# Another dealing of the next tile's attention steps over the parts of the expert heads

## What is computed

```
# forgetting attention, per head (causal)
logits = q k^T * scale + fq[:, None] - log_fcum[None, :]
out = softmax(where(k_pos <= q_pos, logits, -inf)) v
# stick-breaking attention, per head
z = q k^T * scale
log_one_minus = where(k_pos < q_pos, log_sigmoid(-z), 0)
rest = reverse_cumsum(log_one_minus) - log_one_minus
out = where(mask, exp(log_sigmoid(z) + rest), 0) v
x = x + gt1 * (concat(norm(fox), norm(stick)) @ w_out)
# expert layer, per token t and expert head h
u = expert_down[e[t, h, 0:16]]          # gathered rows, by the ids
act = gelu(x u) * gate
x = x + gt2 * sum(act * expert_up[e[t, h, 0:16]])
```

## Time and profile before

| | us |
|---|---|
| three runs, median | 2913.8 |
| the profiled execution's own time | 2913.59 |
| its span in the trace | 2911.8 |
| A1 (30 parts), from 1461.62 | 154.3 |
| A2, from 1826.85 | 167.0 |
| A3, from 2201.24 | 167.4 |

### The profile page before, as it was taken

How to read it: one execution, slowest core, us unless ns; L and a number is a source line. 1 busy time by engine, 2 the same in 40 slices (tenths; PEclk the granted TensorE clock), 3 DMA queues, 4 the chain that set the end, 5 groups by cost and what they waited for, 6 DMA issues and landing times.

```text
span 2911.8 us, 29792 instructions
## 1 busy us (share of the span) xinstructions
PE 2233.5 (77%) x10060; PEld 1001.9 (34%) x10060; DVE 1537.3 (53%) x3500; ACT 840.6 (29%) x1822; POOL 591.3 (20%) x588
## 2 busy tenths in 40 slices
PE   5997999887878874999877667887668876675554
PEld 2444434532222222755632123422234322321110
DVE  3987843500000003201387676777667877677764
ACT  3105301110010002311255322764226652132221
POOL 1000000000000001000134333333333433344442
PEclk9999999898998997999977788988889988887768
DMA  9784545299999997122579999899998999999997
GB/s 369 269 196 131 184 161 232 106 387 405 411 415 404 407 406 302 46 71 76 193 288 411 420 415 421 339 378 411 413 421 348 386 401 407 421 421 421 421 421 294
DMA packets 155968, 948.43 MB, mean 326 GB/s; under 512 B 18522, under 2 KB 50312, under 8 KB 65982
## 3 DMA queue, kind: packets, MB, share of 16 engines
q0 software_dynamic: 78704, 556.90, 47.1%
q1 hardware_dynamic: 68224, 381.17, 34.1%
q10 hardware_dynamic: 8910, 8.75, 0.9%
HBM read 914.99 MB, written 31.77 MB: 325 GB/s over the span
## 4 chain that ended last, share of the span: by engine, by line
PE 40%; DMA 32%; DVE 16%; ACT 5%; issue 4%; POOL 1%; SPq 0%; DVEq 0%; ACTq 0%; POOLq 0%
PE bank L2038 14%; DMA ring<-in_w_exp_up 12%; DMA ring<-in_expert_pair,ids 9%; DMA arena_h<-in_expert_pair,ids 8%; PE bank L2658 7%; PE bank L2044 6%; PE bank L2320 5%; DVE ring L1985 5%; DMA ring<-in_w_in 2%; DVE arena_h L1985 1%; POOL ring L944 1%; ACT L1374 1%; ACT arena_w L1376 1%; PE bank L2603 1%; PE bank L2463 1%
## 5 line engine op out<-in xcount | busy, mean ns | idle before, releaser
L2658 PE MATMUL bank<-ring,arena_w 128*32 128x512 f32 x1668 | 580.1, 740 | 378.3 <-ACT arena_w L1376 377.9
L944 POOL DMA_INDIRECT ring<-in_expert_pair,ids x417 | 444.3, 1065 | 1100.0 <-PE bank L2658 704.3
L2038 PE MATMUL bank<-arena_h,ring 128*128 128x128 f32 (+2 forms) x1264 | 366.5, 451 | 4.6 <-ACT arena_h L1185 3.2
L2658 PEld LDWEIGHTS bank<-ring,arena_w 128*32 128x32 f32 x1668 | 101.8, 123 | 704.6 <-ACT arena_w L1376 494.9
L2320 PE MATMUL bank<-ring,arena_h 128*64 128x512 f32 x1056 | 273.7, 678 | 73.8 <-DMA ring<-in_w_exp_up 72.4
L1985 DVE CUSTOM_DVE_ANT_0 ring<-ring,arena_h 128x1024 f32<-128x1024 f32 x232 | 279.9, 1225 | 91.5 <-DMA ring<-in_expert_pair,ids 66.2
L1985 DVE CUSTOM_DVE_ANT_0 ring<-ring 128x1024 f32<-128x1024 f32 x185 | 224.7, 1225 | 85.3 <-DMA ring<-in_expert_pair,ids 78.8
L1709 DVE TENSOR_TENSOR arena_q<-arena_q,bank 128x256 f32<-128x256 f32 x32 | 13.5, 421 | 473.2 <-ACT arena_q L1122 473.2
L2038 PEld LDWEIGHTS bank<-arena_h,ring 128*128 128x128 f32 x1264 | 205.8, 198 | 157.2 <-issue 121.6
L1374 ACT ACTIVATE arena_w<-arena_w 128x2 f32<-128x2 f32 x256 | 52.0, 203 | 648.8 <-DVE arena_w L1985 648.1
L2320 PEld LDWEIGHTS bank<-ring,arena_h 128*64 128x64 f32 x1056 | 88.8, 155 | 256.2 <-issue 204.6
(11 more groups left out here) (468 smaller groups left out, 2948.3 us busy)
## 6 DMA issues: line engine op xcount, KB each, us to landing
ring<-in_w_exp_gate SPq DMA_DIRECT2D x33, 2048.0 KB, 19.7
ring<-in_w_exp_up SPq DMA_DIRECT2D x33, 2048.0 KB, 24.1
ring<-in_w_exp_down SPq DMA_DIRECT2D x33, 2048.0 KB, 24.9
ring<-in_w_mod SPq DMA_DIRECT2D x12, 2048.0 KB, 15.3
ring<-in_w_in SPq DMA_DIRECT2D x12, 2048.0 KB, 12.7
ring<-in_w_ada SPq DMA_DIRECT2D x12, 2048.0 KB, 8.5
ring<-in_w_query SPq DMA_DIRECT2D x24, 1024.0 KB, 9.2
ring<-in_w_out SPq DMA_DIRECT2D x12, 1024.0 KB, 9.4
```

Source lines behind the costliest of these rows:

```text
L944: pool.indirect_dma_start(pair[pair_of(m)], None, A["expert_pair_2"], bass.IndirectOffsetOnAxis(ap=ids[n % 2][:, r:r + 1], axis=0)).then_i ...
L2038: mm = pe.matmul(dst, w[:, c, at], rhs[:, c, :], start=(c == 0), stop=(c == chunks - 1))
L2658: mm = pe.matmul(bank[4 + half][at, :], sel_q[:, n % 2, k0 + j, :], pair[pair_of(m + j)][:, D + 512 * half:D + 512 * half + 512], start=Fa ...
```

## The change

Where `planned` dealt all steps evenly over 30 parts, it now deals the steps below ST_FOX over the first 21 parts (STICK_PARTS) and the twelve softmax steps over the nine behind them. The later steps keep their parts.

```diff
-        ATTEND_PARTS = 30
+        ATTEND_PARTS, STICK_PARTS = 30, 21
...
             for k in range(first, ST_NORM):
-                at = (k - first) * ATTEND_PARTS // (ST_NORM - first)
+                if k < ST_FOX:
+                    at = (k - first) * STICK_PARTS // (ST_FOX - first)
+                else:
+                    at = STICK_PARTS + (k - ST_FOX) * (ATTEND_PARTS - STICK_PARTS) // (ST_NORM - ST_FOX)
                 plan[at // PARTS][at % PARTS].append(k)
```

## The result

The changed kernel takes 2940.41 us (median of six runs, 2937.2 to 2949.86) where the kernel before took 2916.67 us on the same chip (2895.74 to 2925.29). The two medians differ by 23.7 us, or 0.8%. The ratio on record, which is not the quotient of the medians, is 1.0095 with a 95% interval of 1.0066 to 1.0124: slower, clear of the noise. The forecast was 2903.5 us with a range of 2889 to 2918; the measured time lies outside it.

What follows compares the result with a forecast made beforehand. The gathers at 421 GB/s set the floor, with DVE late in A2 and A3. Against 2913.6 us, -2 (A1) -7.2 +1 (A2) -5.9 +4 (A3) = -10.1 us gave 2903.5 us, range 2889 to 2918.

Steps and rivals of the forecast that it cites:

- The bound: A part's two gathers last 4.98 us at 421 GB/s, the floor; in A2 and A3 a late DVE holds them back.
- The stretches between, parts 30 to 63: Between A2 and A3 the gathers were to stay at 418 GB/s over some 207 us.
- Parts 0 to 15: First halves: A2 from 92.4 to 85.2 us (7.2 less), A3 from 94.1 to 88.2 us (5.9 less).
- The `spread` waits: DVE's waits for the `spread` matmuls in parts 0 to 15, 4.5 us in A2 and 2.3 in A3, were to go.
- A1: Tile 0, width 256: parts 1 and 4 lose their step, 2 us less, bounds 0 and 4.
- Parts 16 to 29: Second halves: A2 76.2 us (1.6 more, 1 counted), A3 80.6 us (7.3 more, 4 counted).
- scores take 2.0 us: PE's time for a softmax step's scores in crowded parts: 2.0 us in part 24, 2.1 in part 21, widths scaled for A3.
- The sentence in the prediction on the clock: Thinner parts 0 to 20 see 1.2 GHz more often, 4.5 and 2.3 us `spread` waits stay; 2910.3 us, within chance 0.27.
- Part 29: Transposes of part 27's second step wait for ACT's copy, delaying the last weighted sum: 1.5 us in A2, 2.0 in A3.
- all of them beside other work: Ten ACT table loads of 1.28 us go, 12.8 us of ACT, lying beside other work.
- The stock of buffers: Eight buffers are 19.9 us of gathers; some 3 us of DVE's lag in A3, parts 16 to 29, may be free.
- The slower one: PE at low clock bounds the nine crowded parts; A2 and A3 lose 10 us more each: 2923.5 us, chance 0.13.

Runs made afterwards that it cites:

- e3_warm: Changed kernel plus two matmuls of zeros on PE in each of parts 16 to 20 of A1 to A3; 2936.08 us.
- e1: Changed kernel with another table for A2 and A3: stick-breaking steps over parts 0 to 17, one softmax step in each of parts 18 to 29; 2912.37 us.
- e2: Stick-breaking steps where the kernel before has them, softmax steps where the changed kernel has them (21 to 29); 2947.95 us.
- e4: Changed kernel with the eight score steps one each in parts 20 to 27 and the last four steps in pairs in 28 and 29; 2922.60 us.
- e5: Changed kernel with the first softmax step moved to part 20, so part 21 keeps one; 2940.92 us.
- e8: Changed kernel with its last four steps one each in parts 27 to 30, undoing the pair of part 27; 2928.97 us.
- e6: Kernel before with step 20, the last with scores, moved from part 24 to part 23 in A2 and A3; 2913.81 us.
- e7: Against the kernel before, in A2 and A3: scores one each in parts 16 to 23, none in 24, last four steps in 25 to 28; 2912.39 us.
- e9: Against the kernel before: scores in parts 15 and 17 to 23, last four steps in 25 to 28, one step to a part; 2906.13 us, ratio 0.9967.

## Why the prediction was wrong, point by point

**The bound: right.** The gathers at 421 GB/s set the floor, and whatever makes DVE late in A2 and A3 ends in the time. All three tiles' differences add up to 23.9 us. The stretches between, parts 30 to 63, were to stay and grew by 2.8 and 0.7 us.

**Parts 0 to 15: right in size.** Forecast 85.2 us in A2 and 88.2 in A3; measured 84.8 and 89.0. The first windows were to stand at 345 GB/s or more and stand at 345 and 345. The `spread` waits were to go and are 0.6 and 1.4 us. By lost time, each window's length times (1 - rate/421), the first halves lose 10.4 and 12.5 us where the earlier trace rows gave 16.9 and 18.0. A1 gave its 2.9 us in the first half and took back 3.3 in the second, where I had counted nothing.

**Parts 16 to 29: the term that failed.** Forecast 76.2 and 80.6 us, measured 84.8 and 94.2. DVE's own work was as counted, within 0.7 us; its waits were to be 11.1 and 13.7 us and were 19.0 and 27.6. By place:

| waits, us | A2 forecast | A2 measured | A3 forecast | A3 measured |
|---|---|---|---|---|
| part 21, both | 1.8 | 2.57 + 3.12 | 2.4 | 3.50 + 3.84 |
| part 24, both | 7.2 | 3.55 + 2.35 | 8.2 | 4.72 + 6.36 |
| part 25 | 0 | small | 0 | 3.53 |
| part 29 | 1.5 | 3.6 | 2.0 | 3.7 |
| other scores | 0.6 | 1.6 | 1.1 | 1.6 |
| gathers | 0 | 2.2 | 0 | 0.3 |

Two terms of this sum were mis-sized. The larger one is the time of the scores in the double parts, "scores take 2.0 us" (2.1 in part 21, 4/3 of it in A3). I took it from one row at full clock and used it for parts that PE would reach after five thin ones. The other is the wait of part 29, below. In part 21 the timeline shows 3.87 us for the scores in A2. In A3, where the same matmuls are 512 wide, it is 4.72 us (2329.02 to 2333.74) against the 2.8 of the forecast, and DVE's two waits there are

```profile
2333.91 0.69 DVE L1821 TENSOR_REDUCE smx<-bank 128x1 f32<-128x512 f32 x1 [3.50 <-PE bank L2468]
2338.63 0.69 DVE L1821 TENSOR_REDUCE smx<-bank 128x1 f32<-128x512 f32 x1 [3.84 <-PE bank L2468]
...
2357.61 0.69 DVE L1821 TENSOR_REDUCE smx<-bank 128x1 f32<-128x512 f32 x1 [4.72 <-PE bank L2468]
2364.85 0.69 DVE L1821 TENSOR_REDUCE smx<-bank 128x1 f32<-128x512 f32 x1 [6.36 <-PE bank L2468]
2373.85 0.69 DVE L1821 TENSOR_REDUCE smx<-bank 128x1 f32<-128x512 f32 x1 [3.53 <-PE bank L2468]
```

with part 24 (third and fourth row) and part 25 (last row) behind them. e3_warm showed that the clock made this: with PE kept busy in parts 16 to 20 the scores took 2.10 us in A2 and part 21 stood as forecast, and part 24 took 9.2 and 10.0 us. In these traces the clock is most of the miss. By the medians it is not: e3_warm's is 4.3 us under the changed kernel, while one step to a part (e1) is 28 us under it. What the runs show most firmly is that the pairs make the loss; how much of it the clock makes in the typical execution stays open.

The sentence in the prediction on the clock was on the right track and at the wrong place. I had weighed that thinner parts 0 to 20 would see the 1.2 GHz level more often, and had let it cost only the `spread` waits, which went away. It was the parts behind the thin ones that paid. In part 21 the granted clock was 0.55 and 0.54 after; in the experiments with fewer softmax scores in parts 16 to 20 than the kernel before and nothing added there (e1, e2, e4, e5, e8) it was 0.50 to 0.86 in A2 and A3, once 1.00; in the kernel before and in e6, e7 and e9, which have at least as many, it was 1.00 each time. How low it gets differs from one execution to the next: e8 has the same steps as the changed kernel up to part 26 and had 0.71 and 0.50. The Trainium skill (TensorE: Matmul & The Clock Gate, What's actually happening) says that the slow level is the default and activity lifts it. The trace agrees, 0.68 and 0.72 in parts 21 to 23 after and 1.00 in e3_warm, which differs by added activity alone. My reason against this rival, a window with PE busy 0.89 of the time and a clock of only 0.80, was no reason: at a low clock the same matmuls take longer, so a high busy share is also what a low clock looks like. And that window is a mean of two levels: its parts 16 to 20 had 0.71, its parts 21 to 23 1.00.

**Part 29: the mechanism was named, the size was not.** The weighted sum of part 27's second step was to come 1.5 us late and came 3.6 us late. PE in A2:

```profile
1994.35 0.87 PE L2476 MATMUL bank<-ident,ring 128*128 128x128 f32 x3 [4.43 <-ACT ring L1287]
...
2002.77 0.88 PE L2484 MATMUL bank<-arena_v,ring 128*128 128x64 f32 x6
```

and DVE, at the end of part 29:

```profile
2003.77 0.20 DVE L1828 RECIPROCAL rinv<-ssum 128x8 f32<-128x8 f32 x1 [3.58 <-PE bank L2484]
```

The copy for which PE stood still for 4.43 us is behind a table load and an exponent in ACT's list (and behind the Gelu of that part, with a load of its own at 1989.63):

```profile
1991.71 1.28 ACT L1398 ACT_TABLE_LOAD   x1
1993.01 0.58 ACT L1278 ACTIVATE ring<-bank,smx 128x384 f32<-128x384 f32 x1
...
1993.71 0.49 ACT L1287 ACTIVATE ring<-bank 128x384 f32<-128x384 f32 x1
```

So a table load can lie on the path, in a double part. I had placed all of them beside other work. Ten of them are gone (ACT's busy time fell from 840.6 to 827.5 us, 13.1 us), and no wait of DVE shows a gain from that, presumably because they were in parts without that turn-taking. No run took out a load by itself, so what the loads cost in part 29 is not shown.

**The stock of buffers: not there.** I had let 3 us of DVE's lag in A3 and 0.6 in A2 be free. In A3 the lag was 20.9 us and the gathers lost 21.3 more than before (25.5 against 4.2), all of it. In A2 the lag was 10.2 us and 8.1 were lost by the windows; some 2 us were covered, and the stretch behind took 2.8 us longer.

**The rivals.** The slower one was the right mechanism in the main: PE bounds the crowded parts at a low clock, and PE and DVE take turns in the double ones. Its own sum for parts 21 to 29 was 55 + 6 = 61 us in A2 and 65 + 6 = 71 us in A3; measured 60.7 and 71.8. Its point of decision was a mean clock of some 0.8 in parts 21 to 29; by the windows it was 0.81 in A2 and 0.77 in A3. (That the earlier trace rows show 0.80 only once is wrong: A1's first window has it too.) It took 20 us more than forecast in the two second halves, and it was 22.2. It had 0.13 of the chance, too little, with the clock left out where it costs most. And it was priced at 2923.5 us, 17 short of the median. That PE has too much to do in the crowded parts is not the whole either: with the same matmuls one step to a part, over twelve parts, e1 was not to be told from the kernel before. In the profiled execution (2946.3 us) the ledger closes: 2903.5 + 22.2 (waits) + 3.9 (not free) + 4.0 (tile 0: +2.0 instead of -2) + 3.5 (parts 30 to 63 of tiles 1 and 2) + 0.4 (first halves) + 8.9 (ahead of A1 and behind tile 2) = 2946.4. The last 8.9 us are not the change's, as far as I can see.

**What stays open.** The gain of the first half alone was not run without a denser second half; e1 is the nearest, with half of it. Why e5 and e3 show less in their medians than in their traces was not settled: the clock that one execution meets in part 21 need not be that of another, and each kernel has one trace.

## What to carry to other kernels

A step's time on PE is not a property of the step: before work is moved from thin parts into crowded ones, ask at which clock PE will arrive there, and take the duration from rows that follow a similar quiet. Avoid two steps whose engines answer each other (PE, ACT, PE) between the same pair of waits: one to a part lengthened a whole second half by 2.3 and 2.6 us (e1), while with the pairs part 21 took 6.4 and 8.6 us more than before, part 24 1.7 and 6.8, part 29 4.5 and 4.6. And look at a step's place within a repeating unit, not only at how evenly the steps are dealt: without scores part 24 took 2.3 us instead of 8.1 and 8.4 (e6). Ask then what comes back behind it; of that gain little was left in the time.

## What the runs showed of the hardware

- In the changed kernel (A2), after parts with PE busy 16.0 of 24.1 us and an idle stretch of 3.37 us, two 384-wide fp32 matmuls took 1.65 us instead of 0.91, and this lasted through both heads' scores; the granted clock of the three parts was 0.68. This is not fixed by the busy share ahead: in e2_softmax_only PE was busy 14.51 of 24.73 us in the same five parts, its idle stretch before part 21 was 1.64 us, and the three parts behind had 0.90.
- In e3_warm two useless matmuls in each of five parts brought the clock to 1.00 there and in the three parts behind, at little cost to DVE: parts 16 to 20 took 24.56 and 23.23 us with them, 24.10 and 22.48 without.
- Two dependent steps without any scores in one part held DVE up for 6.63 us, with PE idle for 4.65 of it (e4_one_at_21_24, A2).
- The gathers held 419 to 423 GB/s on the one core that ran, over parts 16 to 29 of A2 in e6_step20_at_23 (66.8 us).
